# Second attention of a two-layer trunk: the product of probabilities and inverse sums goes from VectorE to GpSimd

## The reference, cut to what matters

```python
def softmax_with_sink(s, sink):
    ...
    return jax.nn.softmax(jnp.concatenate([s, col], axis=-1), axis=-1)[..., :-1]
...
        s_lat = jnp.where(band, jnp.einsum('bqkgd,bskd->bkgqs', qi, kb).astype(jnp.float32), -jnp.inf)
        s_ctx = jnp.einsum('bqkgd,bskd->bkgqs', qi, k_ctx).astype(jnp.float32)
        p = softmax_with_sink(jnp.concatenate([s_lat, s_ctx], axis=-1), sink).astype(v.dtype)
        return (jnp.einsum('bkgqs,bskd->bqkgd', p[..., :span], vb)
                + jnp.einsum('bkgqs,bskd->bqkgd', p[..., span:], v_ctx))
```

## Time and profile before

| What | Value |
|---|---|
| median of 3 runs | 1193.26 us (1192.82 to 1193.74) |
| span of the profiled execution, first to last instruction | 1190.9 us |
| what lies around the span, median less span | 2.4 us |
| TensorE busy over the span | 1151.1 us, 97% |
| VectorE busy | 688.0 us, 58% |
| ScalarE busy | 490.6 us, 41% |
| GpSimd busy | 8.5 us, 1% |
| mean granted TensorE clock | 0.997 of full speed |
| second attention, first turn to first matmul of the output projection | 888.8 to 940.4 us |

### The profile page before, as it was taken

The page is one execution under the profiler, slowest core; times in us unless marked ns, Lnnn a source line. Parts: engine busy times, 40 slices in busy tenths (PEclk is TensorE's granted clock), DMA queues, the critical chain, the costliest instruction groups (busy, mean ns, idle before and its releaser), DMA issues.

```text
span 1190.9 us, 17575 instructions
## 1 busy us (share of the span) xinstructions
PE 1151.1 (97%) x7174; PEld 930.1 (78%) x7174; DVE 688.0 (58%) x1156; ACT 490.6 (41%) x750; POOL 8.5 (1%) x16
## 2 busy tenths in 40 slices
PE   4999999999999999999999999999999999999998
PEld 3777766777588888888887767899565798998997
DVE  3499987854542333333223358887789645554455
ACT  4343235643443332222222333367268635443442
POOL 0100000000000000000000000000000000000000
PEclk9999999999999999999999999999999999999999
DMA  9745654025553213332223564244140157655551
GB/s 359 264 142 170 210 201 171 1 68 216 178 176 106 82 60 98 114 121 92 79 80 114 187 216 139 78 138 142 37 132 12 39 179 244 212 177 177 191 167 67
DMA packets 117838, 167.73 MB, mean 141 GB/s; under 512 B 4766, under 2 KB 102664, under 8 KB 113544
## 3 DMA queue, kind: packets, MB, share of 16 engines
q1 hardware_dynamic: 117334, 166.23, 41.9%
q10 hardware_dynamic: 433, 0.51, 0.1%
HBM read 164.37 MB, written 1.05 MB: 139 GB/s over the span
## 4 chain that ended last, share of the span: by engine, by line
PE 76%; DVE 18%; ACT 3%; issue 2%; DMA 1%; SPq 0%; ACTq 0%; DVEq 0%; POOL 0%
PE acc L2021 18%; PE acc L2022 18%; PE acc L2023 18%; DVE Y L1331 6%; DVE w_lo L617 2%; PE acc L2083 2%; PE acc L2085 1%; PE acc L2084 1%; PE pmod L1958 1%; PE p L2370 1%; PE p L2369 1%; PE p L2371 1%; PE p L1906 1%; DVE sm L1411 1%; DMA xin<-in_ctx 1%
## 5 line engine op out<-in xcount | busy, mean ns | idle before, releaser
L617 DVE TENSOR_TENSOR w_lo<-raw,w_hi 128x1024 fp32r<-128x1024 f32 x226 | 253.8, 1164 | 242.4 <-ACT w_hi L607 242.1
L607 ACT ACTIVATE w_hi<-raw 128x1024 fp32r<-128x1024 f32 (+1 forms) x228 | 216.9, 999 | 425.6 <-PE acc L2023 351.9
L2021 PE MATMUL acc<-Hhi,w_hi 128*128 128x512 f32 (+1 forms) x976 | 333.5, 342 | 6.1 <-POOL ptap L659 4.5
L2022 PE MATMUL acc<-Hlo,w_hi 128*128 128x512 f32 (+1 forms) x976 | 331.2, 339 | 0.0
L2023 PE MATMUL acc<-Hhi,w_lo 128*128 128x512 f32 (+1 forms) x976 | 331.2, 339 | 0.0
L2021 PEld LDWEIGHTS acc<-Hhi,w_hi 128*128 128x128 f32 x976 | 185.6, 190 | 31.7 <-issue 9.1
L2023 PEld LDWEIGHTS acc<-Hhi,w_lo 128*128 128x128 f32 x976 | 185.5, 190 | 20.3
L2022 PEld LDWEIGHTS acc<-Hlo,w_hi 128*128 128x128 f32 x976 | 185.6, 190 | 20.0
L2021 PE MATMUL acc<-hid_hi,w_hi 128*128 128x512 f32 x248 | 97.9, 395 | 0.1
L2022 PE MATMUL acc<-hid_lo,w_hi 128*128 128x512 f32 x248 | 96.6, 390 | 0.0
L2023 PE MATMUL acc<-hid_hi,w_lo 128*128 128x512 f32 x248 | 96.6, 389 | 0.0
(11 more groups left out here) (375 smaller groups left out, 1546.6 us busy)
## 6 DMA issues: line engine op xcount, KB each, us to landing
raw<-in_mod_w SPq DMA_DIRECT2D x48, 1024.0 KB, 5.2
raw<-in_ffn_w_in SPq DMA_DIRECT2D x44, 1024.0 KB, 5.1
raw<-in_od_w_in SPq DMA_DIRECT2D x15, 1024.0 KB, 5.3
raw<-in_ev_w_in SPq DMA_DIRECT2D x10, 1024.0 KB, 7.6
raw<-in_ffn_w_out SPq DMA_DIRECT2D x12, 768.0 KB, 4.5
raw<-in_od_w_out SPq DMA_DIRECT2D x8, 1024.0 KB, 5.4
raw<-in_ffn_w_out SPq DMA_DIRECT2D x8, 1024.0 KB, 5.1
raw<-in_ev_w_out SPq DMA_DIRECT2D x8, 768.0 KB, 6.4
```

The lines of the kernel that those rows point to most:

```text
L607: nc.scalar.activation(w_hi[:, w % 2, c0:c1], raw[:, r % RAW_SLOTS, c0:c1], ACT.Copy)\
L617: nc.vector.tensor_tensor(w_lo[:, w % 2, c0:c1], raw[:, r % RAW_SLOTS, c0:c1], w_hi[:, w % 2, c0:c1].bitcast(F32), ALU.subtract).then_inc( ...
L2021: mm(outs[m], hi[:, j, cols], xh, start=(first and j == 0), stop=False)
L2022: mm(outs[m], hi[:, j, cols], xl, start=False, stop=False)
```

## The change

GpSimd gets a loop of its own over the pairs at the end of its program: it waits for the pair's inverse sums and does the two products. VectorE's reciprocal now counts `invC_ready` in place of VectorE's own chain semaphore, and VectorE's two products and the wait ahead of them are gone. `pC_norm`, on which TensorE's turn waits, is counted by GpSimd. Shapes, types, buffers and all other orders stay.

```diff
@@ -668,6 +668,12 @@
             nc.gpsimd.memset(Xb[:, 4:6, 2 * LAT:2 * T], 0.0).then_inc(s("parts_zero"), 1)
+
+            for u in range(PAIRS):
+                pool.wait_ge(s("invC_ready"), u + 1)
+                for e in range(2):
+                    p_ = probC[:, u % 3, e, :]
+                    nc.gpsimd.tensor_scalar(p_, p_, smC[:, u % 3, 4, e:e + 1], None, ALU.mult).then_inc(s("pC_norm"), 1)
 
@@ -1852,7 +1858,7 @@
                 if u is not None:
                     step.need(summed)
-                    inverse = step.mark(V_.reciprocal(su[:, 4, :], su[:, 6, :]))
+                    V_.reciprocal(su[:, 4, :], su[:, 6, :]).then_inc(s("invC_ready"), 1)
@@ -1860,11 +1866,6 @@
                                             op0=ALU.mult, op1=ALU.add).then_inc(s("skC_ready"), 1)
-                if u is not None:
-                    step.need(inverse)
-                    for e in range(2):
-                        p_ = probC[:, u % 3, e, :]
-                        V_.tensor_scalar(p_, p_, su[:, 4, e:e + 1], None, ALU.mult).then_inc(s("pC_norm"), 1)
```

## The result

| | before | changed |
|---|---|---|
| median | 1193.4 us | 1211.24 us (4 runs, 1209.97 to 1211.78) |
| span of the profiled execution | 1190.9 us | 1209.5 us |
| mean granted TensorE clock | 0.997 | 0.992 |

The account below looks back on a forecast made before the run. VectorE was taken to pace the first nine turns, TensorE the later ones. First half +2.6 us and later half +1.2 gave +3.8 on 1193.26, so 1197.1 us; range 1191.6 to 1202.2 us.

Parts of the forecast that it names:

- Step 1: VectorE loses both products: -0.80 us per iteration in the first half of the pairs, worth nothing in the later half.
- Step 2: Duration d of each GpSimd product: 0.78 us taken, bounds 0.53 (fill) and 1.29 (tensor_tensor).
- Step 3: GpSimd's wait for VectorE's reciprocal: its 0.16 us record plus 0.06 for the signal, bounded by nothing and 0.2.
- Step 5: Sum over the pairs: first half +2.6 us from VectorE's iterations, later half 0.23 per pair, +1.2; total +3.8 us.
- GpSimd as the bound: GpSimd's products, d near 1.29 without exclusion, delay some 13 pairs: +6.4 us, 1199.7 us; chance 0.10.
- Both: d near 1.29 with exclusion, in both halves of the pairs: +11.9 us, 1205.2 us; chance 0.13.
- Step 4: GpSimd and VectorE two-SBUF-input instructions exclude each other for whole instructions: L1861 waits 0.67 us, turns released 0.65 later.
- The sign that step 4 named: L1867 starting some 0.7 us behind its predecessor, not 0.07, with GpSimd's first product ending just then, shows exclusion.

Follow-up runs that it names:

- half: Changed kernel with GpSimd multiplying only the first 256 of the 512 columns of each head: 1197.04 us, ratio 1.0034 to the kernel before.
- copy: Changed kernel with a GpSimd copy in place of each product, probabilities not normalised: 1192.63 us, ratio 0.9994 to the kernel before.
- probes: Kernel before plus eight forms of GpSimd work, twice each, on an unused buffer behind the attention; two such kernels, one execution each: 1193.67 and 1192.28 us.
- split: VectorE multiplies the first head of each pair and GpSimd the second, against both on GpSimd in the changed kernel: 1196.27 us, ratio 1.0029 to before.
- tensor_tensor: Changed kernel with the same GpSimd product written as a tensor_tensor with the inverse sum broadcast along the columns: 1203.1 us, ratio 1.0079 to before.

## Why the prediction was wrong, by its steps

**Step 1, VectorE loses 0.80 us per pair: right, but hardly won.** Its busy time falls by 5.6 us and not by 16 x 0.80 = 12.8, since L1867 now takes 0.43 us more in most pairs, and it waits for the mask, 11.4 us in all.

**Step 2, the duration: this failed.** The step took d = 0.78 us and called 1.29 a bound from above, since the tensor_tensor "reads one tensor more". The product takes 1.56, so that a pair's products end 2.05 us late and not 0.65. The half and the copy show that this length is what costs: at 0.92 us the time is +3.7, at 0.61 it isn't told apart from before. The bound assumed that fewer inputs can't cost more; the probes show the reverse, 1.57 against 1.29, and 1.04 for the same product with the inverse broadcast. The copy, at 0.61, was near the lower bound, so the error belongs to this form of instruction. The Trainium skill (GPSIMD Engine Reference, section 4.1, Engine selection) calls one-input work roughly line-rate. The copy's 0.61 us comes near that, against 0.40 for VectorE's product of the same shape; tensor_scalar, 1.56 us, doesn't. The 1.29 stands against 0.69 for VectorE's own tensor_tensor of that shape (L1292).

**Step 3, the wait: right.** GpSimd starts 0.26 us behind the reciprocal's start, for the 0.22 taken.

**Step 5, the loop formula: right, for the later half.** It said: late by L, slack 0.2, half of the rest per pair. With the products' end at R + 0.26 + n x d and R + 1.33 before, and 3.19 us as the spacing before, it gives the spacing of turns 8 to 12, which all six kernels run at full clock:

| Kernel | n x d | L | formula | measured |
|---|---|---|---|---|
| before | | 0 | | 3.19 |
| copy | 2 x 0.62 | 0.17 | 3.19 | 3.18 |
| split | 1 x 1.56 | 0.49 | 3.33 | 3.38 |
| half | 2 x 0.92 | 0.77 | 3.47 | 3.46 |
| tensor_tensor | 2 x 1.04 | 1.01 | 3.59 | 3.66 |
| changed | 2 x 1.56 | 2.05 | 4.11 | 4.10 |

The rival "GpSimd as the bound" had the mechanism: with d = 1.56 and L = 2.05 it is 0.92 x 13 = 12.0, less 2.6, plus 0.7: +10.1 us. It was priced for 1.29 at most. The rival "Both", priced at 1.56 in the same way (odd iterations +2.21, even ones +1.87), gives about +16 (its p = 6, put at +0.5 in the prediction, is +0.97 by the same rule at 1.29), nearer to the 17.8, but it needs L1867 held for 1.45 us, and it is held for 0.43.

Against the 13.9 us that aren't the clock's, 3.8 are left. Some 1.6 of them lie between turns 2 and 6, which in the changed kernel stand 4.50 us apart at full clock and not 4.10:

```profile
902.42 0.29 PE L2713 MATMUL acc<-maskB,identB 128*128 128x128 bf16 x2
903.04 1.21 DVE L1850 TENSOR_REDUCE smC<-acc 128x2 f32<-128x1024 f32 x1
904.64 3.51 POOL L676 TENSOR_SCALAR probC<-probC,smC 128x512 f32<-128x512 f32 x2 [1.32 <-DVE smC L1861]
...
911.32 0.28 PE L2713 MATMUL acc<-maskB,identB 128*128 128x128 bf16 x2
912.59 1.22 DVE L1850 TENSOR_REDUCE smC<-acc 128x2 f32<-128x1024 f32 x1
```

Where VectorE is free, the reduction starts 0.32 us behind the mask (898.61 behind 898.29). Here it starts 0.30 and 0.95 us later than that, behind VectorE's work on `mixC` and `yN`, and two products take 3.51 us instead of 3.12 beside that work: 1.64 us, for 18.02 - 4 x 4.10 = 1.62. So the first half has a source of delay of its own, as step 5 said, but by another way than the iterations that it added up. Of what is left, part is that the last turns, which nothing covers, lose 2.87 and 0.83 us in the table of turns, clock included, for the 0.7 taken. The remainder wasn't divided further.

**Step 4, the exclusion: half right.** Both directions exist. But a tensor_scalar of GpSimd holds VectorE's next two-input instruction for 0.58 - 0.15 = 0.43 us, not for d - 0.11 = 1.45, and 256 columns hold it for 0.21: the hold goes with the columns but is a quarter of the instruction. A copy holds the negation for 0.38 of 0.61, a tensor_tensor for 0.82 of 1.04. The sign that step 4 named came out in part: L1867 is long, but it ends long before GpSimd's first product does. The Trainium skill (SBUF — State Buffer, section "SBUF: two separate sides") has whoever starts first hold the shared ports for the whole instruction: the tensor_tensor is close to that, the tensor_scalar is not. Why the negation is held beside the one and the instruction behind it beside the other stays open. In the later half of the changed kernel the hold is covered, since VectorE waits for TensorE there (1.33 us at 927.22); in the tensor_tensor kernel the first half runs at VectorE's pace, holds included (14.86 of 15.00 us busy).

**Left out: the clock.** "The clock is full in all of them" was read from the kernel before and carried over. The forecast had no case in which it falls. Waits of 1.8 to 2.4 us ahead of a turn came with stretches at 1.2 GHz, and filling them gave 3.9 us back. The half kernel, near the length that was forecast, waits 1.4 us at most and keeps its full clock; so this miss follows from that of step 2.

The "half" kernel came out at +3.7 against the forecast's +3.8, at a duration near the one assumed. That is partly luck: its product is longer than 0.78 and holds VectorE for less, and the time lies elsewhere. Its turn 8 is 1.35 us late, where the forecast had +2.6 for the first half; turns 8 to 12 add 1.05, near the forecast's 0.23 per pair; and the last three turns add 1.2, for which the forecast charged nothing. No kernel tried is faster than before by more than its interval.

## What to carry to other kernels

A product that sits in a loop from TensorE over VectorE and back costs what it ends later than the loop's slack allows, once each time round (here every two pairs), even on an engine that is idle for 95% of the span. Write the loop with each engine's measured duration, and compare the end of the moved work with the end of what it replaces. Time GpSimd's instruction in the exact form that will be used, and try the same result in other forms (1.56 against 1.04 us here). When the path gets longer, give the forecast a case in which TensorE's new gaps lower its clock, and ask which engine GpSimd's instruction holds meanwhile.

## What was not expected of the hardware

- On GpSimd, 128 x 512 f32: multiplication by one value per partition 1.56 us, two full tensors 1.29, one tensor and a broadcast 1.04, copy 0.61, fill 0.52.
- Beside a fill of 1.81 us on GpSimd, which reads nothing, a 128 x 2 instruction of VectorE took 1.79 us instead of 0.17.
- Eight transposes per pair with nothing useful in them made a kernel 3.9 us faster, and a delay of 0.45 us at each pair's start on GpSimd made one 11.8 us slower, with the mean clock down from 0.992 to 0.985.
